# Top-k rounds of a sparse attention spread over the steps by their cost, with the gate banks emptied first and the masks formed on ScalarE

## What is computed

```python
proj = hn @ w_in[l]
aq, ak, av, bq, bkv, iq, ik, iw, gates = jnp.split(proj, IN_SPLITS, axis=-1)
gates = jax.nn.sigmoid((gates + b_gates[l]).astype(jnp.float32)).astype(h.dtype)
o_a = sliding_window_sink_attention(aq, ak, av, sinks[l], bias_a)
...
# indexed_sparse_mla, for a block of 128 queries
logits = jnp.einsum('bqhd,bsd->bqhs', qi, ik)
score = jnp.einsum('bqhs,bqh->bqs', jax.nn.relu(logits).astype(jnp.float32), wi.astype(jnp.float32))
score = jnp.where(admissible[None], score, -jnp.inf)
_, sel = lax.top_k(score, topk)                 # topk = 128 here
...
s = jnp.where(valid[:, :, None, :], s + bias, NEG)
pr = jax.nn.softmax(s, axis=-1)
...
mixed = gate_a * (o_a @ w_branch_a[l]) + gate_b * (o_b @ w_branch_b[l])
```

## Time and profile before

| | us |
|---|---|
| median of 3 runs | 1500.18 |
| lowest and highest | 1499.02, 1501.77 |
| the profiled execution | 1499.58 |
| its span, first to last instruction | 1497.9 |
| TensorE busy in the span | 1477.7 |
| VectorE busy | 957.0 |
| ScalarE busy | 605.1 |
| GpSimd busy | 221.2 |

### The profile page before, as it was taken

How to read it: one execution, slowest core, us unless ns; L and a number is a source line. 1 busy time by engine, 2 the same in 40 slices (tenths; PEclk the granted TensorE clock), 3 DMA queues, 4 the chain that set the end, 5 groups by cost and what they waited for, 6 DMA issues and landing times.

```text
span 1497.9 us, 21903 instructions
## 1 busy us (share of the span) xinstructions
PE 1477.7 (99%) x8042; PEld 1233.0 (82%) x8042; DVE 957.0 (64%) x1707; ACT 605.1 (40%) x1061; POOL 221.2 (15%) x194
## 2 busy tenths in 40 slices
PE   8999999999999999999999999999999999999998
PEld 7867776878788888898898777777787888888987
DVE  6668897565795587377854372424667855873865
ACT  5235436534443243244511374444344433432434
POOL 2013324340000000000003663322400000000000
PEclk9999999999999999999999999999999999999999
DMA  7624320033333333332323202121333333333322
GB/s 174 152 65 146 117 57 1 23 104 99 98 99 99 101 97 99 98 104 71 107 85 84 56 2 85 57 64 36 102 95 99 99 99 112 89 95 98 113 70 100
DMA packets 250309, 132.99 MB, mean 89 GB/s; under 512 B 21225, under 2 KB 247653, under 8 KB 250222
## 3 DMA queue, kind: packets, MB, share of 16 engines
q1 hardware_dynamic: 247998, 123.92, 29.2%
q0 software_dynamic: 2144, 7.77, 1.8%
q10 hardware_dynamic: 80, 0.14, 0.0%
HBM read 129.67 MB, written 6.38 MB: 91 GB/s over the span
## 4 chain that ended last, share of the span: by engine, by line
PE 91%; DVE 5%; DMA 1%; issue 1%; ACT 1%; POOL 0%; SPq 0%; DVEq 0%; ACTq 0%
PE psL L2050 50%; PE psS L2073 12%; PE psL L2236 11%; PE psS L2050 5%; PE psT L2245 2%; PE psL L2371 1%; PE psS L2541 1%; PE psL L2496 1%; PE psS L2344 1%; PE psS L2519 1%; PE psS L2475 1%; DVE acc L1479 1%; PE psS L2286 1%; DVE st L1478 1%; PE psS L2476 0%
## 5 line engine op out<-in xcount | busy, mean ns | idle before, releaser
L775 ACT ACTIVATE wh<-stage 128x1024 fp32r<-128x1024 f32 (+3 forms) x232 | 225.4, 971 | 366.2 <-PE psL L2050 260.0
L2050 PE MATMUL psL<-hn,wh 128*128 128x512 f32 x1104 | 347.9, 397 | 0.4 <-DVE ft L1733 0.4
L2050 PEld LDWEIGHTS psL<-hn,wh 128*128 128x128 f32 x1104 | 204.8, 188 | 50.3 <-issue 3.7
L1208 DVE TENSOR_TENSOR wl<-stage,wh 128x1024 fp32r<-128x1024 f32 (+1 forms) x157 | 187.6, 1195 | 78.9 <-ACT wh L775 78.5
L2050 PE MATMUL psL<-hn,wl 128*128 128x512 f32 x552 | 217.1, 393 | 0.0
L2050 PE MATMUL psL<-hid,wh 128*128 128x512 f32 x680 | 209.6, 390 | 1.4 <-DVE wl L1208 1.4
L636 POOL TENSOR_TENSOR wl<-stage,wh 128x1024 fp32r<-128x1024 f32 (+2 forms) x75 | 140.0, 1867 | 278.5 <-ACT wh L775 278.5
L2236 PE MATMUL psL<-hn,wh 128*128 128x512 f32 x496 | 166.9, 418 | 2.2 <-DVE tmp L1468 2.0
L2050 PEld LDWEIGHTS psL<-hid,wh 128*128 128x128 f32 x680 | 127.4, 188 | 28.9 <-DVE wl L1208 2.2
L2050 PE MATMUL psL<-hid,wl 128*128 128x512 f32 x340 | 132.3, 389 | 0.0
L2050 PEld LDWEIGHTS psL<-hn,wl 128*128 128x128 f32 x552 | 103.8, 188 | 23.5
(11 more groups left out here) (438 smaller groups left out, 2644.3 us busy)
## 6 DMA issues: line engine op xcount, KB each, us to landing
stage<-in_w_in SPq DMA_DIRECT2D x54, 512.0 KB, 3.8
stage<-in_w_ffn_gate SPq DMA_DIRECT2D x22, 512.0 KB, 3.8
stage<-in_w_ffn_up SPq DMA_DIRECT2D x22, 512.0 KB, 3.8
stage<-in_w_ff_gate SPq DMA_DIRECT2D x22, 512.0 KB, 3.8
stage<-in_w_ff_up SPq DMA_DIRECT2D x22, 512.0 KB, 3.8
stage<-in_w_out SPq DMA_DIRECT2D x16, 512.0 KB, 4.0
stage<-in_w_ffn_down SPq DMA_DIRECT2D x16, 512.0 KB, 4.0
stage<-in_w_ff_down SPq DMA_DIRECT2D x16, 512.0 KB, 4.1
```

Of the source, the lines that this page charges most:

```text
L775: act.activation(wh[:, b, 0:n], stage[:, b, 0:n], ACT.Copy).then_inc(hi[b], 1)
L1208: v.tensor_tensor(wl[:, b, 0:n], stage[:, b, 0:n], wh[:, b, 0:n].bitcast(F32), ALU.subtract).then_inc(lo[b], 1)
L2050: ins = pe.matmul(dst, w[:, b, k * P:(k + 1) * P], x[:, part, k, c0:c1], start=k + n == 0, stop=k == kc - 1 and n == 2)
```

## The change

Three things change, all in the stage `window1`:

1. `SELECTION`, worked out once when the kernel is built, says which rounds fall to which step. A round is weighed by its row length plus 226, a step by the number of its gate quarters and, from step 8 on, a little more. A step has between 0 and 3 rounds; the last block's last round lies in step 30.
2. On VectorE `gate_part` comes before `top_rounds` in each step.
3. The mask of a block is no longer formed on VectorE but on ScalarE, two steps after the block's last round, as relu(acc x 2^-27 + 1e30) in bf16: 0 where a score was taken, 1e30 elsewhere. GpSimd subtracts it from the bias where it added it before. A new semaphore, `top_ok`, tells ScalarE that a block's rounds are done; the constant 1e30 is a new tile of 128x1, filled by GpSimd at the start. VectorE waits for all four masks before it overwrites `acc` with the values of the latent attention.

```diff
@@ the table
+def selection_steps():
+    rounds = [(i, n) for i in range(NB) for n in range(TOPK // 8)]
+    cost = [META + P * (i + 1) + 226 for i, _ in rounds]
+    quarters = [GATE_QUARTERS[1][j] - (0 if j else 4) for j in range(NB * NH)]
+    room = [1.2 * q + (0.1 if j < NH else 0.2) for j, q in enumerate(quarters)]
+    room[-1] = 0
+    steps, n = [], 0
+    for j in range(NB * NH):
+        steps.append([])
+        while n < len(rounds) and sum(cost[:n]) * sum(room) < sum(cost) * sum(room[:j + 1]):
+            steps[j].append(rounds[n])
+            n += 1
...
+SELECTION = selection_steps()
+SELECTED = {i: j for j, rounds in enumerate(SELECTION) for i, n in rounds if n == TOPK // 8 - 1}
@@ GpSimd, at the start
+            own.link(pool.memset(mask[:], MASK))
@@ GpSimd, mask_bias
-                pool.tensor_tensor(biasM[:, j % 4, 0:K], biasB[:, h, NKEY - K:NKEY], selm[:, i, 0:K], ALU.add).then_inc(biasM_ok, 1)
+                pool.tensor_tensor(biasM[:, j % 4, 0:K], biasB[:, h, NKEY - K:NKEY], selm[:, i, 0:K], ALU.subtract).then_inc(biasM_ok, 1)
@@ ScalarE
+            def mask_block(i):
+                K = META + P * (i + 1)
+                act.wait_ge(top_ok, i + 1)
+                act.activation(selm[:, i, 0:K], acc[:, i, 0:K], ACT.Relu, bias=mask[:, 0:1], scale=2.0 ** -27).then_inc(sel_ok, 1)
...
                 gate_tanh(1, j)
+                for i in range(NB):
+                    if SELECTED[i] == j - 2:
+                        mask_block(i)
                 if 2 <= j < len(units) + 2:
                     take_turn(p, j - 2, NEAR, PTa)
@@ VectorE, top_rounds
-                blk, n = divmod(j, ROUNDS // 2)
-                K = META + P * (blk + 1)
-                for _ in range(2):
-                    dv.link(v.max(best, acc[:, blk, 0:K]))
-                    dv.link(v.match_replace(acc[:, blk, 0:K], best, acc[:, blk, 0:K], TAKEN))
-                if n == ROUNDS // 2 - 1:
-                    v.tensor_scalar(selm[:, blk, 0:K], acc[:, blk, 0:K], TAKEN / 2, NEG, ALU.is_gt, ALU.mult).then_inc(sel_ok, 1)
+                for i, n in SELECTION[j]:
+                    K = META + P * (i + 1)
+                    dv.link(v.max(best, acc[:, i, 0:K]))
+                    taken = v.match_replace(acc[:, i, 0:K], best, acc[:, i, 0:K], TAKEN)
+                    if n == TOPK // 8 - 1:
+                        taken.then_inc(top_ok, 1)
+                        v.wait_ge(top_ok, i + 1)
+                    else:
+                        dv.link(taken)
@@ VectorE, the steps
+                gate_part(1, j)
                 if j < len(units):
                     top_rounds(j)
-                gate_part(1, j)
@@ VectorE, after the stage
+            v.wait_ge(sel_ok, NB)
             values_even(0)
```

More of the change, by code:

```diff
@@ L47 @@
 TAKEN = -3e38
+MASK = 1e30
 TOPK = 128
@@ L232 @@
 GATE_QUARTERS = {1: [5] + [1] * 7 + [2] * 26, 2: [4] + [2] * 24 + [1] * 10 + [2]}
+def selection_steps():
[10 more added lines that the diff above has]
+            n += 1
+    assert n == len(rounds)
+    return steps
+SELECTION = selection_steps()
+SELECTED = {i: j for j, rounds in enumerate(SELECTION) for i, n in rounds if n == TOPK // 8 - 1}
 GATE_START = {l: [n for n, c in enumerate(q) for _ in range(c)][0::4] for l, q in GATE_QUARTERS.items()}
@@ L296, in build @@
         neglam = keep("neglam", [P, 1])
+        mask = keep("mask", [P, 1])
         subg = keep("subg", [P, 1])
@@ L478, in build @@
         lg_mm, lg_taken, lg_used = [sem(n) for n in "lg_mm lg_taken lg_used".split()]
-        sel_ok = sem("sel_ok")
+        sel_ok, top_ok = sem("sel_ok"), sem("top_ok")
         th_ok = [sem(f"th_ok{b}") for b in range(2)]
@@ L1470, in _ @@
             best = st[:, 9, :]
-            ROUNDS = TOPK // 8
             def top_rounds(j):
-                blk, n = divmod(j, ROUNDS // 2)
-                K = META + P * (blk + 1)
-                for _ in range(2):
-                    dv.link(v.max(best, acc[:, blk, 0:K]))
-                    dv.link(v.match_replace(acc[:, blk, 0:K], best, acc[:, blk, 0:K], TAKEN))
-                if n == ROUNDS // 2 - 1:
-                    v.tensor_scalar(selm[:, blk, 0:K], acc[:, blk, 0:K], TAKEN / 2, NEG, ALU.is_gt, ALU.mult).then_inc(sel_ok, 1)
+                for i, n in SELECTION[j]:
[7 more added lines that the diff above has]
+                        dv.link(taken)
             def biased(p, u, tile, scores, bias, most, col):
```

## The result

| | before | after |
|---|---|---|
| median of 12 runs | 1499.39 us | 1504.52 us |
| lowest and highest | 1498.32, 1501.77 | 1502.72, 1507.52 |
| the profiled execution, its span | 1499.58, 1497.9 | 1504.02, 1502.3 |

The changed kernel takes 1.0030 times as long, 95% interval 1.0021 to 1.0038. Its median is 5.1 us higher where 3.6 us of gain were forecast.

The account below looks back on a forecast made before the run. TensorE was taken to bound the kernel, with one stall in window attention. Removing 2.07 us of idle time and 1.55 us of slow stretch from the 1500.18 us median gave 1496.6 us, own range 1495.2 to 1497.9.

Parts of the forecast that it names:

- What bounds the kernel; the stall: TensorE, busy 1477.7 of 1497.9 us, idles 2.07 us at 214.60 behind VectorE's late eviction of tmp; the change removes this.
- the slow stretch: Window attention, 218 to 220 us: granted clock 0.50 right behind the idle time, making one step 1.55 us longer.
- Gate banks first: VectorE, window stage: eviction ahead of two selection rounds moves up by 3.10 us, alone covering the 2.07 us idle time.
- Masks on ScalarE: Window stage: four masks leave VectorE, at most 0.61 us each on ScalarE against 1.07 to spare; cost nothing.
- Rival C: Masks delay ScalarE's bank copies, stopping TensorE in four places: 8.6 us lost less 3.6, 1505.2 us; chance 0.07.
- The held additions: VectorE's remaining additions, window stage: may again be held by GpSimd's port lock, a sink sum 1.57 us against 0.17 free.
- Uneven spread: VectorE's selection rounds over the pairs: lateness at most 2.4 us after 26/27, margin 2.2 us at worst, so TensorE never waits.
- The sum: Whole kernel: 2.07 us of stall and 1.55 of slow stretch, 3.62 together, off the median 1500.18 gives 1496.6 us.
- Rival A: Window stage: the stall goes but the slow stretch does not count, or the clock falls elsewhere: 1498.1 us; chance 0.15.
- Adding 32 bytes to the layout ...: nothing.: Memory layout, under the added memset: the 32 bytes, and subtracting in GpSimd instead of adding, were priced at nothing.
- the rest is untouched: Everything outside the window stage: unchanged, so the gain cannot exceed the stage's 3.62 us.

Follow-up runs that it names:

- the kernel without the shift: Changed kernel with the mask constant in spare bytes behind lam, so every large tile keeps its old address: 1496.25 us, ratio 0.9972.
- The long series: Kernel before with groups of 96 matmuls of 512 columns added at its end, at 13 address settings, each twice: 226.9 to 233.5 ns per matmul.
- the kernel before with the pad ahead of everything: Kernel before with an unused 32-byte tile declared ahead of all others, so weights and moving operands shift together: 1501.19 us, ratio 1.0009.
- the tile first: Changed kernel with only the declaration of the constant mask moved ahead of the first tile: 1496.64 us, ratio 0.9982.
- the kernel before with the same shift: Kernel before with only an unused 32-byte tile ahead of subg, moving gate, hn, mix, hid, xt and all behind: 1508.66 us, ratio 1.0057.
- the first series: Kernel before with 16 groups of 24 matmuls at chosen addresses added at its end; the same group at address 0 took 230.0, then 227.5 ns.
- the last four kernels: Pad ahead of everything (1501.19 us); changed kernel with its tile first (1496.64), with lengthened hn rows (1487.64), with those and xt moved 32 bytes (1486.32).

## Why the prediction was wrong

**What bounds the kernel; the stall.** Right. 2.07 us of idle TensorE and the slow stretch behind it went from the stage, and the kernel without the shift came to 1496.25 where 1496.6 was forecast.

**Gate banks first.** Right, "this alone covers the 2.07 us", as the run of this part alone shows (0.9972). VectorE in order of time: the eviction follows the biased scores at once, where two rounds stood between them in the earlier trace rows.

```profile
206.62 0.48 DVE L1517 CUSTOM_DVE_ANT_0 W3a<-psS,biasA,nsink 128x256 f32<-128x256 f32 x1 [0.29 <-PE psS L2306]
...
207.43 0.69 DVE L1499 TENSOR_TENSOR tmp<-psL,Rk 128x512 f32<-128x512 f32 x1
```

**Masks on ScalarE.** Right that they cost nothing: the third mask is in the shade of the wait for `psT`. Their size was a little low. "At most 0.61 us each" came from a relu on 528 columns; 0.61 is what the mask on 400 columns took, and the one on 528 took 0.72, still less than the 1.07 to spare. ScalarE in order of time:

```profile
187.49 0.61 ACT L906 ACTIVATE selm<-acc,mask 128x400 bf16<-128x400 f32 x1
188.89 0.38 ACT L925 ACTIVATE PTa<-psT 128x256 f32<-128x256 f32 x1 [0.79 <-PE psT L2278]
```

Rival C did not come about: TensorE waits for nothing in the stage. That its price, 1505.2 us, lies 0.7 from the measured 1504.52 is chance. The held additions came too, as foreseen: VectorE's 8 columns take 1.56 us and end at 155.59, GpSimd's subtraction at 155.56, as in the earlier trace rows.

```profile
154.03 1.56 DVE L1523 TENSOR_TENSOR st<-sinkb,negm 128x8 f32<-128x8 f32 x1
```

```profile
153.17 2.39 POOL L658 TENSOR_TENSOR wl<-stage,wh 128x1024 fp32r<-128x1024 f32 x1 [5.26 <-ACT wh L797]
```

The Trainium skill (SBUF — State Buffer, section "SBUF: two separate sides") has VectorE and GpSimd lock a shared pair of ports, and ScalarE never wait. The two rows agree with the lock. With the second half agrees the mask of block 0: it ran on ScalarE from 138.79 to 139.19 us beside GpSimd's subtraction of 137.83 to 140.23, and its 0.40 us lie on one line with the 0.51, 0.61 and 0.72 of the three longer masks, which had no such neighbour. By the same section TensorE never waits on anyone either. The long series had nothing beside it and still came to 233.3 ns, so whatever the address does there, it is not another engine's traffic.

**Uneven spread.** The pairs were bounded by up to 2.4 us of lateness. The worst is behind pair 14/15, which took 9.16 us where 7.7 to 9.1 was reckoned: the scores begun at 159.92, and 0.63 us in the making, were read at 162.25, 1.7 us late where 1.4 was reckoned. Right in the main, but of no use here: the swap alone had already removed the stall.

**The sum.** The term of 1.55 us for the slow stretch is sounder as an average than as an event. In the kernel before with the pad ahead of everything, the same stall of 2.00 us was followed by no slow stretch, and instead by a second wait of 1.09 us. Its stretch of time (granted clock behind POOL), to be read against the earlier trace rows:

```profile
216.00:220.00 4.00, 3.89 (x20) 3.29 (x21) 3.83 (x11) 2.44 (x5) 1.98 (x1) 1.00 0.00 0
```

In the changed kernel the clock fell elsewhere, at 744 us as shown above, and in the one without the shift at 850 us:

```profile
848.00:852.00 4.00, 3.82 (x15) 2.31 (x13) 3.20 (x11) 2.58 (x7) 1.17 (x2) 0.68 0.02 4
852.00:856.00 4.00, 4.00 (x17) 2.81 (x17) 2.52 (x8) 1.97 (x6) 2.46 (x5) 0.50 0.00 0
```

Rival A foresaw this ("or falls elsewhere after the shift"). VectorE is 5 us late at both stalls; in one profile TensorE lost the time to a slow stretch, in the other to a second stop. The medians give 3.6 us of gain without the shift and with the swap alone, and 2.0 with the tile first. Part of this is how many runs of a series had slow stretches. Among runs with a mean clock of 0.997 or more, the same three average 3.0, 3.6 and 3.2 us under the kernel before. So more than the 2.07 of the stall was gained, and the sum of 3.62 is at the upper end of what was measured.

**The step that failed** is one clause: "Adding 32 bytes to the layout ...: nothing." It priced an edit of the layout by what it computes and not by what it moves. It measured 8.1 us in the kernel before (1506.0 - 1497.9). In the changed kernel the way from +4.05 us at 290 us to -4.4 at the end is 8.45. Four pieces of 240 at 1.30 each are 5.2 of it. About 0.9 is the slow stretch at 744 us: from the piece of 108 matmuls to that of 405 the changed kernel took 44.37 us, and the kernel before with the same shift, which has no slow stretch there, 43.43. The rest, some 2.3, lies in the other pieces on `hid` and `mix` (the piece of 219 matmuls from 332 us takes 51.50 us, not 50.93). By the medians, a loss of 8.8 (the shift alone) less a gain of 3.6 is 5.2, and 5.1 was measured. No rival had it, and "the rest is untouched" was true of the instructions and false of their addresses.

## What to carry to other kernels

Work out where each tile lies before and after a change, and treat a new small tile as an edit of every tile behind it: declare it last, first, or in spare bytes. Where TensorE is the bound, look at the distance in bytes between moving operand and weights modulo 256; here choosing it was worth twice as much (7.6 us) as the stall that the change was about (3.6 at most). And when several parts are aimed at one wait, test each alone: the order of two calls did what three edits were made for.

## What the runs showed of the hardware

- In long series, 128x512 matmuls of this kernel (f32r operands, new weights each time) come every 226.7 to 227.6 ns when the moving operand and the weights are 0 bytes apart modulo 256, and every 232.2 to 233.5 ns when 32, 96 or 128 apart. At 16 it is 231.7. At 64 it is 229.0 with the moving operand moved, 233.3 with the weights moved, and either of the two in the kernel itself.
- Short stretches don't always reach the good pace: in the profile of the kernel before, the products on `oA` and `oB`, 12 matmuls at a time at distance 0, come every 226.6 or 226.7 ns in 17 of 32 stretches and every 228.6 to 230.8 in the rest, and the groups of 24 in the first series took 230.0 and 227.5. What decides between them no run shows, so the full rule stays open.
- At 256 columns it is the other way: 119.6 ns for `xt` with `wh` at 0, 116.4 at 32. Why is open, and so is where between 256 and 512 columns it turns.
- In the long series no other engine worked and the DMA share was 0.02 or less, so the difference needs no traffic beside TensorE; which part of the chip makes it no run shows.
- A granted clock of 0.50 for some microseconds came and went between profiles: at 218 us in two with the stall, at 744 in the changed kernel, at 744 and again at 853 to 860 in one with the stall, and between 20 and 1480 us nowhere in three others. In the 18 runs of the kernel before that stand beside the last four kernels, a mean clock of 0.996 goes with 1501.3 us on average (3 runs), one of 0.997 or 0.998 with 1498.7 (15 runs).
